# Four of the low-part subtractions of a float32 kernel's weights, put on GpSimd instead of VectorE

## The reference, cut to what matters

```
h = rmsnorm(x, norm_mix_g)
proj = h @ w_in                      # q, k, v, forget gate, conv inputs
q, k, v = heads(proj[..., 0:512]), heads(proj[..., 512:1024]), heads(proj[..., 1024:1536])
attn = forgetting_attention(q, k, v, log_f)
conv = conformer_conv(proj[..., OFF_C:], ...)      # GLU, causal depthwise conv of width 31, layernorm, swish
x = x + concat(rmsnorm(attn), conv) @ w_out
mem_n = rmsnorm(mem, mem_norm_g)
k, v = split(mem_n @ w_mkv)          # columns 0:512 of w_mkv are the unit mem_kv0
x = x + cross_attention(rmsnorm(x), k, v) @ w_mo
...                                  # mixture of 32 experts, then the whole second block
```

## Time and profile before

| | |
|---|---|
| median of 3 runs | 1398.08 us (1397.04 to 1401.07) |
| profiled execution | 1398.36 us, of which the profile's span is 1396.3 us |
| busy in the span | TensorE 85%, its weight loads 59%, VectorE 43%, ScalarE 27%, GpSimd 1% |
| chain of work that ended last | TensorE 58%, transfers 28%, VectorE 9% |

### The profile page before, as it was taken

The page is one execution under the profiler, slowest core; times in us unless marked ns, Lnnn a source line. Parts: engine busy times, 40 slices in busy tenths (PEclk is TensorE's granted clock), DMA queues, the critical chain, the costliest instruction groups (busy, mean ns, idle before and its releaser), DMA issues.

```text
span 1396.3 us, 16589 instructions
## 1 busy us (share of the span) xinstructions
PE 1190.9 (85%) x7132; PEld 820.2 (59%) x7132; DVE 593.8 (43%) x993; ACT 375.1 (27%) x571; POOL 13.7 (1%) x23
## 2 busy tenths in 40 slices
PE   5999999986675566657657999999999999999997
PEld 5977868541221212212117988888867647998863
DVE  3799543320010100101004498874756425664443
ACT  1352422100000000000002456433364213554322
POOL 2000000000000000000001000000000000000000
PEclk9997999988888988888888999999989999999999
DMA  9432273299999999999991534433531134445440
GB/s 342 183 132 110 109 313 131 101 389 428 428 428 428 428 428 426 428 428 428 428 426 50 185 124 152 148 121 127 202 155 61 37 138 162 187 186 189 182 151 30
DMA packets 26971, 332.57 MB, mean 238 GB/s; under 512 B 3185, under 2 KB 3473, under 8 KB 5009
## 3 DMA queue, kind: packets, MB, share of 16 engines
q1 hardware_dynamic: 25760, 328.47, 58.8%
q0 software_dynamic: 1136, 3.02, 0.7%
HBM read 330.43 MB, written 1.05 MB: 237 GB/s over the span
## 4 chain that ended last, share of the span: by engine, by line
PE 58%; DMA 28%; DVE 9%; issue 2%; ACT 2%; SPq 0%; DVEq 0%; ACTq 0%
PE ps L493 10%; PE ps L543 9%; DMA ring<-in_w_gate 9%; PE ps L512 9%; DMA ring<-in_w_up 9%; PE ps L1083 6%; DMA ring<-in_w_down 6%; PE ps L567 6%; PE ps L801 3%; DMA arena<-in_w_up 2%; PE ps L456 2%; DMA ring<-in_units 2%; PE ps L912 2%; DVE arena L1260 1%; DVE parts L1216 1%
## 5 line engine op out<-in xcount | busy, mean ns | idle before, releaser
L1216 DVE TENSOR_TENSOR parts<-ring,parts 128x2048 fp32r<-128x2048 f32 x76 | 173.5, 2290 | 155.8 <-ACT parts L1889 155.5
L1889 ACT CAST parts<-ring 128x2048 fp32r<-128x2048 f32 x76 | 144.4, 1904 | 177.2 <-PE ps L493 73.5
L512 PE MATMUL ps<-parts 128*128 128x512 f32 x768 | 180.5, 395 | 0.0
L493 PE MATMUL ps<-parts 128*128 128x256 f32 x1344 | 164.9, 285 | 3.0 <-DVE parts L1216 3.0
L493 PEld LDWEIGHTS ps<-parts 128*128 128x128 f32 x1344 | 163.4, 194 | 3.6 <-DVE parts L1216 2.1
L512 PEld LDWEIGHTS ps<-parts 128*128 128x128 f32 x768 | 144.9, 190 | 30.8 <-issue 1.1
L801 PE MATMUL ps<-ring,arena 128*32 128x512 f32 x688 | 101.3, 719 | 71.6 <-DMA ring<-in_w_gate 43.5
L543 PE MATMUL ps<-ring,arena 128*128 128x512 f32 x320 | 141.4, 599 | 4.8 <-issue 3.4
L1487 DVE TENSOR_TENSOR arena<-arena,ps 128x512 f32<-128x512 f32 x32 | 22.0, 688 | 262.4 <-PE ps L838 262.3
L801 PEld LDWEIGHTS ps<-ring,arena 128*32 128x32 f32 x688 | 21.0, 119 | 147.0 <-DMA ring<-in_w_gate 52.5
L543 PEld LDWEIGHTS ps<-ring,arena 128*128 128x128 f32 x320 | 60.5, 192 | 77.6 <-issue 76.2
(11 more groups left out here) (322 smaller groups left out, 1226.4 us busy)
## 6 DMA issues: line engine op xcount, KB each, us to landing
ring<-in_units SPq DMA_DIRECT2D x43, 2048.0 KB, 8.2
ring<-in_w_up SPq DMA_DIRECT2D x22, 2048.0 KB, 40.3
ring<-in_w_gate SPq DMA_DIRECT2D x21, 2048.0 KB, 41.4
ring<-in_w_down SPq DMA_DIRECT2D x20, 2048.0 KB, 41.7
ring<-in_units SPq DMA_DIRECT2D x31, 1024.0 KB, 5.0
arena<-in_w_down SPq DMA_DIRECT2D x12, 2048.0 KB, 40.5
arena<-in_w_gate SPq DMA_DIRECT2D x11, 2048.0 KB, 40.2
arena<-in_w_up SPq DMA_DIRECT2D x10, 2048.0 KB, 40.8
```

Of the source, the lines that this page charges most:

```text
L493: mm = nc.tensor.matmul(banks[f][:, half * T:half * T + T], w[:, k, at:at + P], v[:, 4 * h + k, :], start=h + half + k + n == 0, stop=h + ...
L512: mm = nc.tensor.matmul(banks[t], v[:, 4 * h + k, t * P:t * P + P], w[:, k, :], start=h + k + n == 0, stop=h == 1 and k == 3 and n == 2)
L1216: step(V.tensor_tensor(rest_half(name, h), split_half(name, h), w_high[stage][h].bitcast(F32), ALU.subtract), f"{stage}_rest_ready", wait= ...
L1889: step(S.copy(w_high[stage][h], split_half(name, h)), f"{stage}_high_ready", wait=False)
```

## The change

The low parts of two units, k (u = 1) and mem_kv0 (u = 3), are subtracted by GpSimd. VectorE's `split_rest` returns without doing anything for these, and nothing else moves in its order. GpSimd gets the four subtractions after its first transfers, each behind a wait for the high part; they raise a semaphore of their own, `pool_rest_ready`, and TensorE waits for that one for the two units. The count that it waits for with the other units is reduced by the units taken out.

```
+        on_pool = ["k", "mem_kv0"]
...
                 def part_pairs(name, h, high, rest):
                     stage, u = split_at[name]
-                    pe.wait_ge(sem(f"{stage}_rest_ready"), 2 * u + h + 1)
+                    if name in on_pool:
+                        pe.wait_ge(sem("pool_rest_ready"), 2 * on_pool.index(name) + h + 1)
+                    else:
+                        by_others = len([v for v in split_stages[stage][:u] if v in on_pool])
+                        pe.wait_ge(sem(f"{stage}_rest_ready"), 2 * (u - by_others) + h + 1)
...
                     if u < len(split_stages[stage]):
                         name = split_stages[stage][u]
+                        if name in on_pool:
+                            return
...
+                for name in on_pool:
+                    stage, u = split_at[name]
+                    for h in range(2):
+                        pool.wait_ge(sem(f"{stage}_high_ready"), 2 * u + h + 1)
+                        nc.gpsimd.tensor_tensor(rest_half(name, h), split_half(name, h), w_high[stage][h].bitcast(F32),
+                                                ALU.subtract).then_inc(sem("pool_rest_ready"), 1)
+
                 filled_by(pool, "route1")
```

## The result

The changed kernel took 1407.39 us (median of 5 runs, 1404.86 to 1409.66) against 1399.32 us for the kernel before in the same runs (1397.04 to 1401.07). The ratio is 1.0057, with a 95% interval from 1.0038 to 1.0076: some 8 us. The forecast was 7.8 us slower and 1405.8 us, with 0.58 on slower.

The account below looks back on a forecast made before the run. VectorE was taken to set the pace for some 40 us up to mem_kv1 at 103.41 us, TensorE afterwards. 5.8 + 0.4 + 1.6 = 7.8 us on 1398.1 gave 1405.8 us, range 1395.8 to 1409.

Parts of the forecast that it names:

- A GpSimd subtraction takes 4.6 us: Each moved subtraction, on GpSimd: twice VectorE's 2.29 us, as if its two inputs were fetched one after the other.
- Full standstill: VectorE's instructions with two SBUF inputs stand still for a whole GpSimd subtraction; chance 0.53, own range 1402.5 to 1409 us.
- k costs TensorE 0.8 us: At k's first half: GpSimd works until 60.0 us, TensorE could start at 59.2, so it starts 0.8 us late.
- Taps 5 to 7 end near 70.6 us: VectorE's twelve-instruction convolution block beside k: ends at 70.6 us instead of 69.4, 1.2 us late.
- mem_kv0's first half makes TensorE wait 1.8 us: Before mem_kv0: GpSimd works until 89.8 us, TensorE wants the half at 88.0 and waits 1.8 us.
- mem_kv1's first half 5.8 + 0.4 us late: VectorE's subtraction for mem_kv1 ends at 109.05 instead of 103.27 us, plus 0.4 for GpSimd waiting on running VectorE instructions.
- Lower clock on mem_kv1, 1.6 us: After TensorE idles about 7 us before mem_kv1, its products run partly at 1.2 of 2.4 GHz, costing 1.6 us.
- The sum: Whole kernel: 5.8 + 0.4 + 1.6 = 7.8 us slower, on 1398.1 us.
- Every later step is late by the same amount: After mem_kv1's start near 109.5 us, the delay is carried to the end and no later wait takes it up.
- no hindrance: VectorE keeps its pace and is spared four subtractions: 1396.8 us, or 1393.5 with 2.29 us subtractions; chance 0.31.
- VectorE first: GpSimd gets in only where VectorE waits, making mem_kv1 14.4 us late: 1412.5 us; chance 0.07.
- hindered by half: Both engines slow each other instead of standing; mem_kv1 is ready at 105 us: 1400 us; chance 0.09.

Follow-up runs that it names:

- the spare work: Kernel before, VectorE keeping all its subtractions, plus four same-size GpSimd subtractions at the same moments whose result nobody uses; 1.0115, 1412.89 us.
- k alone: Only the unit k subtracted on GpSimd, mem_kv0 back on VectorE, against the kernel before; 1.0025, 1402.17 us.
- mem_kv0 alone: Only the unit mem_kv0 subtracted on GpSimd, k back on VectorE, against the kernel before; 1.0037, 1402.53 us.
- the two kernels that had no wait left before it: Kernel before, all on VectorE, three subtractions moved ahead of taps, without and with the last two taps behind the softmaxes; 0.9997 and 0.9986.
- e6_spare_memset: Kernel before plus four GpSimd instructions that only write zeros into a free page, at the moments of the four subtractions; 1.0004, 1399.89 us.

## Why the prediction was right, point by point

- *A GpSimd subtraction takes 4.6 us.* Its rows last 4.76 to 4.91 us, and 5.37 for the first, beside whose start three of VectorE's taps ran on. Without the waiting it took 4.42 to 4.47 us. That is 0.15 us below my 4.6, which came from doubling VectorE's time and not from a row, so its nearness is partly luck; the Trainium skill's 4497 ns (GPSIMD Engine Reference, Performance versus the Vector engine) is nearer. The 0.4 us that I added for waiting on running taps, for all four together, was measured as 0.9 for the first subtraction and 0.3 to 0.4 for each of the others.
- *Full standstill.* Right, and shown apart from everything else by the spare work (1.0115) and by rows of 4.80 us. The reading of the earlier trace rows pointed the right way, but it was thin: one instruction of 0.42 us more, beside transfers being issued and not beside elementwise work.
- *k costs TensorE 0.8 us.* This term was mis-sized. The wait was 1.85 us, since GpSimd's first instruction started 0.1 us after the cast and took 5.37 and not 4.6, and in the profiled execution another 1.6 us was lost to a clock of 0.72 behind it, which I had charged only before mem_kv1. v started 3.6 us late instead of 0.9. k alone measured 3.5 us, where my walk had 1.2 on VectorE and nothing for the clock: its trace shows 2.1 us at mem_kv1's start and 1.3 us of slower products there.
- *Taps 5 to 7 end near 70.6 us.* They ended at 70.3, or 69.8 on the axis of before.
- *mem_kv0's first half makes TensorE wait 1.8 us.* Measured 1.97, although k's lateness was off by 2.4 us: it moved TensorE and GpSimd alike.
- *mem_kv1's first half 5.8 + 0.4 us late.* In the whole change 7.8 us. k's part was 3.6 us instead of 1.2, too small by 2.4; mem_kv0's was 4.3 us (the same in the trace of mem_kv0 alone) instead of 5.0, too large by 0.7.
- *Lower clock on mem_kv1, 1.6 us.* Measured 2.1 (14.02 against 11.89 us), after 6.88 us of waiting, forecast as about 7.
- *The sum.* 7.8 us forecast, 8.1 us between the medians. That they meet is partly luck. In the profiled execution the same terms add up to 9.9 us at mem_kv1's end: k 2.4 more than forecast, mem_kv0 0.7 less, the clock 0.5 more. That execution is 2.3 us above its median, and how the median one divides its 8.1 us no trace shows. (1398.1 + 7.8 is 1405.9; the forecast's 1405.8 is a slip in the last digit.)
- *Every later step is late by the same amount.* Right within about 1 us. With nothing taken off, TensorE was 10.5 us late at mem_kv1's end (125.76 against 115.30), 9.6 at mem_kv2's start, 10.5 again at 266 us, the first of GpSimd's later transfers 11.5 (290.12 against 278.63), and the span is 11.3 us longer. No wait further on took the delay up.

The rivals: no hindrance and VectorE first are excluded by the rows, hindered by half by the spare work. Against VectorE first I had argued that its short instructions leave gaps. They do not, they begin every 0.40 us and last 0.47; GpSimd got in all the same, behind the running tap in three of four cases and one or two taps later in the first. What I had not seen while forecasting is the other side of the chain's reading. I found no wait further on in the chain, and rightly for a delay; for a gain there was one, the copy of mem_kv1's last result out of its PSUM bank at 126 us, which kept most of the profit of the two kernels that had no wait left before it.

## What to carry to other kernels

Before elementwise work is moved from VectorE to GpSimd, ask what VectorE executes at that moment: beside work that reads SBUF a GpSimd subtraction cost VectorE its whole length here, so at 4.4 us for 2.29 us spared the move loses wherever such work on VectorE bounds the stage, even if nobody waits for GpSimd's result. Beside VectorE's idle time or its copies out of PSUM the first subtraction cost it 0.9 us. When one engine feeds another from a hand-written list, move the feeding instructions ahead of the filler before looking for another engine, then read TensorE's waits again, since a stall moves to the next consumer of the same list. Price the relief first by leaving the work out: here that run gave 0.9962 for the order as it was, and a better order with all the work in it came out at 0.9958, within the intervals the same.

## What was not expected of the hardware

- With its waits for VectorE taken off, GpSimd takes about 5.2 us to scale 128x2048 float32 (one input), 4.4 us to subtract two different tensors, 3.5 us to subtract a tensor from itself, and 1.81 us to fill one with zeros.
- Beside GpSimd's scaling a tap of VectorE was free again 1.4 us before GpSimd's row ended, while a one-input instruction stood to the end.
- A wait of 1.85 us on TensorE was followed by products at a granted clock of 0.72 in one execution and 1.00 in another. The wait before mem_kv0's second half went both ways too: 1.92 us and then 0.77 in the kernel before, 1.96 us and then 1.00 in e6_spare_memset, with the same order of work on both engines. The waits of nearly 7 us seen here were followed by the lower clock both times (0.58, and 13.56 us for 96 products where 11.75 is usual at 1.00).
